# Starting one of five weight slots 96 bytes into a 128-byte line

## The reference

```python
x = x + attn(rms_norm(x, g1) @ w_in) @ w_out
x = x + relu(rms_norm(x, g2) @ mlp_w1) ** 2 @ mlp_w2     # two such layers
...
u = rms_norm(x, g5) @ w_up                               # third layer
x = x + rms_norm((gelu(conv(u0)) * conv(u1)) @ w_down, g6)
```

## Time and profile before

| what | value |
|---|---|
| median of 3 runs | 1136.49 us (1133.57 to 1137.23) |
| the profiled execution's own time | 1134.4 us |
| its span | 1132.6 us |
| TensorE matmul busy | 1109.1 us (98%) |
| TensorE weight load busy | 1068.6 us (94%) |
| VectorE busy | 786.1 us (69%) |
| ScalarE busy | 587.8 us (52%) |
| GpSimd busy | 140.6 us (12%) |
| mean share of the DMA engines for the weight queue | 52.9% |
| mean granted TensorE clock | 0.995 |

### The profile page before, as it was taken

How to read it: one execution, slowest core, us unless ns; L and a number is a source line. 1 busy time by engine, 2 the same in 40 slices (tenths; PEclk the granted TensorE clock), 3 DMA queues, 4 the chain that set the end, 5 groups by cost and what they waited for, 6 DMA issues and landing times.

```text
span 1132.6 us, 21593 instructions
## 1 busy us (share of the span) xinstructions
PE 1109.1 (98%) x9351; PEld 1068.6 (94%) x9351; DVE 786.1 (69%) x1134; ACT 587.8 (52%) x828; POOL 140.6 (12%) x109
## 2 busy tenths in 40 slices
PE   7999899999999999999999999999999989999998
PEld 6988799999999999999999997999988989999998
DVE  6567488784457566977644689786475889888752
ACT  4477655443336555544433566854366647666531
POOL 4200050001230005000122206201010000111000
PEclk9999999999999999999999999999999999999999
DMA  9943055566654444555555472666464545556551
GB/s 280 276 150 112 1 184 189 186 195 201 200 187 155 154 139 150 186 187 187 186 187 186 132 212 69 200 200 217 131 221 143 188 147 187 186 187 205 186 184 40
DMA packets 195938, 195.72 MB, mean 173 GB/s; under 512 B 9803, under 2 KB 193028, under 8 KB 195844
## 3 DMA queue, kind: packets, MB, share of 16 engines
q1 hardware_dynamic: 193680, 190.53, 52.9%
q10 hardware_dynamic: 2164, 3.82, 1.1%
HBM read 192.86 MB, written 1.47 MB: 172 GB/s over the span
## 4 chain that ended last, share of the span: by engine, by line
PE 94%; DVE 3%; ACT 2%; DMA 0%; issue 0%; DVEq 0%; SPq 0%; ACTq 0%
PE ps_gemm L1727 50%; PE ps_trans L1727 35%; PE ps_score L1804 2%; PE ps_out L1836 2%; PE ps_trans L1821 2%; DVE act_lo L1144 2%; DVE w_lo L1138 1%; PE ps_gemm L1908 1%; PE ps_score L2035 1%; DMA x_in<-in_x 0%; PE ps_out L2035 0%; PE ps_out L2039 0%; PE ps_score L2039 0%; DVE rs L1150 0%; PE ps_score L1770 0%; ACT prob L798 0%
## 5 line engine op out<-in xcount | busy, mean ns | idle before, releaser
L1138 DVE TENSOR_TENSOR w_lo<-raw,w_hi 128x2048 fp32r<-128x2048 f32 (+2 forms) x179 | 408.2, 2289 | 45.2 <-ACT w_hi L753 45.0
L753 ACT ACTIVATE w_hi<-raw 128x2048 fp32r<-128x2048 f32 (+2 forms) x179 | 332.3, 1863 | 175.2 <-DMA raw<-in_mlp_w 95.3
L1727 PE MATMUL ps_gemm<-act_hi,w_hi 128*128 128x256 f32 (+1 forms) x960 | 267.1, 286 | 4.7 <-ACT act_hi L1064 4.4
L1727 PE MATMUL ps_gemm<-act_hi,w_lo 128*128 128x256 f32 (+1 forms) x960 | 259.9, 282 | 0.0
L1727 PE MATMUL ps_gemm<-act_lo,w_hi 128*128 128x256 f32 (+1 forms) x960 | 254.8, 281 | 0.5 <-DVE act_lo L1144 0.4
L1727 PE MATMUL ps_trans<-act_hi,w_hi 128*128 128x256 f32 x688 | 193.1, 281 | 1.9 <-DVE w_lo L1138 1.9
L1727 PE MATMUL ps_trans<-act_hi,w_lo 128*128 128x256 f32 x688 | 193.0, 281 | 0.0
L1727 PE MATMUL ps_trans<-act_lo,w_hi 128*128 128x256 f32 x688 | 192.9, 280 | 0.0
L1727 PEld LDWEIGHTS ps_gemm<-act_hi,w_hi 128*128 128x128 f32 (+1 forms) x960 | 182.1, 192 | 10.2 <-issue 8.2
L1727 PEld LDWEIGHTS ps_gemm<-act_hi,w_lo 128*128 128x128 f32 (+1 forms) x960 | 178.6, 190 | 0.3
L1727 PEld LDWEIGHTS ps_gemm<-act_lo,w_hi 128*128 128x128 f32 (+1 forms) x960 | 173.7, 186 | 2.1 <-DVE act_lo L1144 0.9
(11 more groups left out here) (379 smaller groups left out, 2238.9 us busy)
## 6 DMA issues: line engine op xcount, KB each, us to landing
raw<-in_mlp_w SPq DMA_DIRECT2D x64, 1024.0 KB, 5.4
raw<-in_w_in SPq DMA_DIRECT2D x30, 1024.0 KB, 5.4
raw<-in_w_up SPq DMA_DIRECT2D x24, 1024.0 KB, 5.2
raw<-in_od_w_in SPq DMA_DIRECT2D x12, 1024.0 KB, 5.1
raw<-in_w_down SPq DMA_DIRECT2D x12, 1024.0 KB, 5.2
raw<-in_ev_w_in SPq DMA_DIRECT2D x9, 1024.0 KB, 8.1
raw<-in_w_proj_a SPq DMA_DIRECT2D x8, 640.0 KB, 4.3
raw<-in_ev_w_out SPq DMA_DIRECT2D x4, 1024.0 KB, 5.1
```

Source lines behind the costliest of these rows:

```text
L753: act.activation(w_hi[:, slot, 0:k, 0:n], raw[:, slot, 0:k, 0:n], ACT.Copy).then_inc(hi_done, 1)
L1138: dve.tensor_tensor(w_lo[:, slot, 0:k, 0:n], raw[:, slot, 0:k, 0:n], w_hi[:, slot, 0:k, 0:n].bitcast(F32), ALU.subtract).then_inc(w_ready, 1)
L1727: ins = pe.matmul(dst, lhs, rhs, start=(first and opens and opening), stop=(last and closes and i + 1 == len(order)), skip_group_check=True)
```

## The change

The last slot of all three rings is moved by 96 bytes, and each ring is made 128 bytes longer to hold it. Each slot becomes a tensor of its own. Slots 0 to 3 of `raw` and `w_lo` keep their addresses. Slots 0 to 3 of `w_hi` move by 128 bytes, and so stay on a multiple of 128; slot 4 of `w_hi` moves by 224. All that lies behind the rings moves by 256 bytes. No instruction, wait or loop changes.

```diff
 RING = 5
+SLOT_SHIFT = (0, 0, 0, 0, 96)
...
-    raw = place("raw", [P, RING, KS, NS])
-    w_lo = place("w_lo", [P, RING, KS, NS], F32R, at=base)
-    w_hi = place("w_hi", [P, RING, KS, NS], F32R)
-    nb0 = top[0]
+    slot_at = [i * KS * NS * 4 + SLOT_SHIFT[i] for i in range(RING)]
+    ring = RING * KS * NS * 4 + P
+    raw = [place(f"raw{i}", [P, KS, NS], at=base + o) for i, o in enumerate(slot_at)]
+    w_lo = [place(f"w_lo{i}", [P, KS, NS], F32R, at=base + o) for i, o in enumerate(slot_at)]
+    w_hi = [place(f"w_hi{i}", [P, KS, NS], F32R, at=base + ring + o) for i, o in enumerate(slot_at)]
+    nb0 = top[0] = base + 2 * ring
...
-            sp.dma_start(raw[:, slot, 0:k, 0:n], src).then_inc(raw_in[slot], 16)
+            sp.dma_start(raw[slot][:, 0:k, 0:n], src).then_inc(raw_in[slot], 16)
...
-            act.activation(w_hi[:, slot, 0:k, 0:n], raw[:, slot, 0:k, 0:n], ACT.Copy).then_inc(hi_done, 1)
+            act.activation(w_hi[slot][:, 0:k, 0:n], raw[slot][:, 0:k, 0:n], ACT.Copy).then_inc(hi_done, 1)
...
-            dve.tensor_tensor(w_lo[:, slot, 0:k, 0:n], raw[:, slot, 0:k, 0:n], w_hi[:, slot, 0:k, 0:n].bitcast(F32),
+            dve.tensor_tensor(w_lo[slot][:, 0:k, 0:n], raw[slot][:, 0:k, 0:n], w_hi[slot][:, 0:k, 0:n].bitcast(F32),
                               ALU.subtract).then_inc(w_ready, 1)
...
-                    rhs = w[:, slot, k, 0:n]
+                    rhs = w[slot][:, k, 0:n]
...
-                    lhs = w[:, slot, k, half * P:half * P + mm]
+                    lhs = w[slot][:, k, half * P:half * P + mm]
```

More of the change, by code:

```diff
@@ L535, in a_slab @@
                 for half, c0 in enumerate(starts):
-                    sp.dma_start(raw[:, slot, :, half * P:(half + 1) * P], w_a[:, :, c0:c0 + n]).then_inc(raw_in[slot], 16)
+                    sp.dma_start(raw[slot][:, :, half * P:(half + 1) * P], w_a[:, :, c0:c0 + n]).then_inc(raw_in[slot], 16)
             else:
```

## The result

The changed kernel takes 1147.58 us (median of 5 runs, 1145.75 to 1150.77), against 1136.49 us (1129.38 to 1137.95) for the kernel before beside it. The ratio is 1.0132, with a 95% interval of 1.0089 to 1.0176: slower by 11.1 us in the medians. The forecast was 1122.7 us, in a range of 1112 to 1146. It is 24.9 us too low: the gain of 13.8 us did not come, and the 11.1 us came on top.

What follows compares the result with a forecast made beforehand. TensorE's slab matmuls, at a fast or slow pace, were taken as the bound. The profiled 1134.4 us less 13.8 us gave 1120.6; the run median being 2.1 higher, the forecast was 1122.7 us, range 1112 to 1146.

Steps and rivals of the forecast that it cites:

- What bounds the kernel: TensorE's slab matmuls, 85% of the chain, run at two steady paces, 113.3 and 117.8 ns, 4.5 ns apart.
- DMA, ScalarE, VectorE at nothing: Loads into slot 4 and both engines' passes over it: taken as 0, with 12 us spare to hide slower loads.
- The 0.4 us of a landing: Loads into slot 4: estimated extra landing time if starts off a 256-byte boundary are charged on the written side; hidden.
- The 256 bytes by which all else moves, and the 128 bytes of `w_hi`, keep every offset against a 128-byte line: 0.: Tensors moved by the longer rings: taken to cost 0, unless the moves redraw the paces.
- It is not the address alone ... The pace is held from slab to slab until the stream is disturbed: Slab matmul stretches: equal addresses show both paces; most stretches begin after a pause, six disturbances come without one.
- I take it that slot 4 ends the slow pace, and that a fast stream stays fast: Long unbroken slow stretches: 64 slabs after a first slot-4 slab gain 0.215 us each, 13.8 us; gain given 0.48.
- Slot 4's own reads at 0: TensorE's 1728 matmuls on slot 4: no cost taken; bounds 7.7 us more or 7.8 us less.
- as the 64-byte case is nearest: Reason for zero cost of slot 4's reads: activations starting 64 bytes off a line run at 113.3 ns.
- Rival 2: Fast stretches: slot 4 ends the fast pace instead, losing 11.0 us over 51 slabs, so 1147.5 us; chance 0.22.
- the turn at slab 19: In a_up, the first slot-4 slab of a fast stretch, where the slower-side rival has the fast pace end.
- Rival 1: All stretches: an operand's start does not reach TensorE's pace, every stretch keeps its pace, 1136.5 us; chance 0.30.
- The gap of 262 cycles: TensorE matmuls of 256 columns: the skill's figure, 109 ns, set against the traced 113.3 and 117.8 ns.

Runs made afterwards that it cites:

- second profile: The kernel before, word for word, profiled and timed again: 1131.61 us over ten runs, ratio 0.9970; the profiled execution took 1146.0 us.

## Why the prediction was wrong, point by point

- **What bounds the kernel**, and that two paces 4.5 ns apart share the time of the kernel before: right. The loss is in the pace, 11.3 of 12.3 us, but the changed kernel has slower ones too, 118.3 to 118.5 and 118.9 ns.
- **DMA, ScalarE, VectorE at nothing**: right, by the rows above. The 0.4 us of a landing, an estimate, measured 0.09.
- **"The 256 bytes by which all else moves, and the 128 bytes of `w_hi`, keep every offset against a 128-byte line: 0."** This is the step that failed, and the whole loss is there without any shifted slot. The 256 bytes alone cost nothing that can be measured. The 128 bytes are not: with no slot shifted the kernel is 1.7% slower (1.2 to 2.2), against 1.3% for the whole change. I measured offsets against a line of 128, since the change speaks of one; what counts is the distance between two tensors, modulo 256 here.
- **"It is not the address alone ... The pace is held from slab to slab until the stream is disturbed"**: right for the kernel before, and its second profile shows it more plainly than the first could. But I then took the draws of one profiled execution for the kernel's own.
- **"I take it that slot 4 ends the slow pace, and that a fast stream stays fast": 13.8 us gained.** Wrong for this change, and the second step that failed; it gave the forecast its sign. In the changed kernel slot 4 ends either pace in turn; with the 96 bytes alone it mostly ends neither. It comes true nearly, though not always, for 64 bytes, and the time gains nothing beyond the interval even there.
- **Slot 4's own reads at 0**: wrong. I put them at 0 "as the 64-byte case is nearest", with 4.5 ns and 7.7 us as the upper bound. (Slot 4 holds 35 slabs and not 36, two of them of 30 matmuls: 1644 matmuls and 7.4 us.) In the changed kernel slot 4 is at 118.3 to 118.5 ns, 5 above the fast pace. With the 96 bytes alone it is at 120.0, 6.7 above the fast pace and 2.2 above the slow one. An activation that starts 64 bytes off a line could be fast because the slab was on the line: the difference between the two was 64, and it is the difference that counts.
- **Rival 2, 1147.5 us**, gave the number that was measured, and the turn at slab 19 is in the profile of after. But there slot 4 ends the slow pace as often as the fast one. Its mechanism is a part of it at most: without the 128-byte move the same slot 4 costs nothing net. The agreement of the number is luck.
- **Rival 1**, that starts do not reach TensorE's pace, is wrong as a mechanism: offsets moved the pace from 113.3 up to 120.0 ns. The gap of 262 cycles, which it quotes from the Trainium skill (TensorE: Matmul & The Clock Gate, Back-to-back issue gap), is given there for a matmul by itself, so a pair of load and matmul at 113.3 ns does not speak against that figure.

## What to carry to other kernels

When a matmul stream is the bound, the addresses of its stationary and moving operands relative to each other are part of the tuning: write them down modulo 128 and 256 before and after any change of layout, and change one distance at a time. A pad that was put in for one purpose moves everything behind it. A pace read from one profile may be a draw: profile the same kernel twice before explaining a difference by stages.

## What the hardware showed that I had not expected

All of this is for pairs of a 128 x 128 load and a 256-column float32r matmul at a granted clock of 1.00:

- In the kernel before, a long stretch runs at one of two paces, 113.3 or 117.8 ns, drawn behind a pause (or where the operands change places) and then held for more than thirty slabs where nothing interrupts it. The same program gave 176.1 and 182.6 us for the same two stages.
- The offset between slab and activation modulo 128: 64 allows 113.3 ns. With all slots alike, 32 gives 118.3 (116.7 in r_v and most of f_dn, where the slab moves) and 0 gives 120.0; for a single slot it is the other way round, 120.0 and 118.5, so modulo 128 is not the whole rule. From 64 to 0 for all is 3.2% of the kernel's time.
- The distance between the two weight tensors modulo 256: 0 gives 117.8 ns as the slow pace, 128 gives 118.9 and a kernel 1.7% slower. The rule of the Trainium skill that TensorE has two independent read ports (TensorE: Matmul & The Clock Gate, Step-by-step: what each phase is for) does not lead one to expect that; nor do lines of 16 bytes (SBUF — State Buffer, Door 1: The DMA port swizzle), since every shift here is a multiple of 16.

That loads and matmuls collide in the memory is my guess for the cause. The runs show that these distances matter, not whether or where anything collides. Distances that are not multiples of 32 bytes were not tried, nor was the distance between the high and the low activations.
